# Hybrid decoder step: four prompt units inside each sample attention unit, with the sample keys turned half a unit earlier

## Time and profile before

| | us |
|---|---|
| median of 3 runs | 1231.96 (1231.15 to 1234.93) |
| the profiled execution, its own time | 1237.05 |
| span of the profiled execution | 1235.3 |

### The profile page before, as it was taken

How to read it: one execution, slowest core, us unless ns; L and a number is a source line. 1 busy time by engine, 2 the same in 40 slices (tenths; PEclk the granted TensorE clock), 3 DMA queues, 4 the chain that set the end, 5 groups by cost and what they waited for, 6 DMA issues and landing times.

```text
span 1235.3 us, 23971 instructions
## 1 busy us (share of the span) xinstructions
PE 1068.6 (87%) x9389; PEld 856.7 (69%) x9389; DVE 830.4 (67%) x1497; ACT 264.2 (21%) x588; POOL 350.1 (28%) x378
## 2 busy tenths in 40 slices
PE   5699899999688777778765996999999999999994
PEld 3377577666566555566544875999999999777772
DVE  1647346625778688777639577467676676998958
ACT  0300000012223323232233103332233232100002
POOL 0433123310000000000007005356664665434323
PEclk9799999985899889988886997999999999999997
DMA  8938989863599999998780216375567731413102
GB/s 293 408 135 328 359 329 349 301 238 108 197 366 352 340 344 373 370 327 295 279 305 1 64 38 210 136 266 211 205 232 278 270 105 69 148 57 104 69 19 77
DMA packets 112549, 276.54 MB, mean 224 GB/s; under 512 B 9608, under 2 KB 33174, under 8 KB 108837
## 3 DMA queue, kind: packets, MB, share of 16 engines
q1 hardware_dynamic: 100949, 254.52, 58.2%
q10 hardware_dynamic: 11488, 20.49, 5.0%
HBM read 264.60 MB, written 76.69 MB: 276 GB/s over the span
## 4 chain that ended last, share of the span: by engine, by line
PE 60%; DVE 15%; DMA 11%; ACTq 4%; issue 4%; SPq 2%; ACT 2%; POOL 1%; DVEq 0%; POOLq 0%; PEldq 0%
PE wide L1632 15%; PE wide L1634 15%; PE wide L1633 15%; DMA room<-in_cache_v 3%; PE wide L1768 3%; ACTq L481 3%; PE wide L1712 3%; PE wide L1701 2%; DMA x_sb<-in_cache_v 2%; DMA room<-in_w_ada 2%; DMA ring<-in_w_ada 2%; PE wide L1580 1%; DMA ring<-in_w_down 1%; DVE ring L1202 1%; PE wide L1706 1%
## 5 line engine op out<-in xcount | busy, mean ns | idle before, releaser
L782 POOL TENSOR_TENSOR ring_r<-ring,ring_r 128x1024 fp32r<-128x1024 f32 x70 | 184.6, 2645 | 286.5 <-DVE ring_r L1086 204.3
L1632 PE MATMUL wide<-x_sb_r,ring_r 128*128 128x288 f32 x704 | 211.3, 300 | 8.2 <-DVE ht_r L1108 5.2
L1633 PE MATMUL wide<-ht_r,ring_r 128*128 128x288 f32 x704 | 209.2, 297 | 0.0
L1634 PE MATMUL wide<-x_sb_r,ring_r 128*128 128x288 f32 x704 | 208.4, 296 | 0.0
L1634 PE MATMUL wide<-ring_r,ht_r 128*128 128x512 f32 (+1 forms) x400 | 158.9, 397 | 0.0
L1202 DVE STREAM_TRANSPOSE ring<-ring 128x512 f32<-128x512 f32 x208 | 129.9, 676 | 24.3 <-DMA ring<-in_cache_k 12.2
L1632 PEld LDWEIGHTS wide<-x_sb_r,ring_r 128*128 128x128 f32 x704 | 133.2, 189 | 11.7 <-issue 11.2
L1634 PEld LDWEIGHTS wide<-x_sb_r,ring_r 128*128 128x128 f32 x704 | 134.0, 190 | 0.0
L1633 PEld LDWEIGHTS wide<-ht_r,ring_r 128*128 128x128 f32 x704 | 133.6, 190 | 0.0
L1632 PE MATMUL wide<-ring_r,x_sb_r 128*128 128x512 f32 (+1 forms) x240 | 98.2, 409 | 10.1 <-DVE ht_r L1108 8.7
L770 POOL COPY x_sb<-ring 32x128 f32<-32x128 f32 x64 | 18.4, 287 | 286.4 <-PE wide L1768 284.3
(11 more groups left out here) (231 smaller groups left out, 1892.8 us busy)
## 6 DMA issues: line engine op xcount, KB each, us to landing
ring<-in_cache_k SPq DMA_DIRECT2D x128, 256.0 KB
out_wks<-in_cache_win_k SPq DMA_DIRECT2D x8, 4080.0 KB, 18.9
out_wvs<-in_cache_win_v SPq DMA_DIRECT2D x8, 4080.0 KB, 19.3
ring<-in_w_up SPq DMA_DIRECT2D x22, 1024.0 KB, 7.1
room<-in_w_ada SPq DMA_DIRECT2D x8, 2048.0 KB, 10.5
ring<-in_cache_win_k SPq DMA_DIRECT2D x16, 1024.0 KB
ring<-in_w_in SPq DMA_DIRECT2D x6, 2048.0 KB, 10.7
x_sb<-in_cache_win_v SPq DMA_DIRECT2D x40, 256.0 KB
```

The lines of the kernel that those rows point to most:

```text
L782: nc.gpsimd.tensor_tensor(rest, w, high.bitcast(F32), ALU.subtract).then_inc(wl_rest, 1)
L1632: nc.tensor.matmul(out, left[0], right[0], start=first, stop=False)
L1633: nc.tensor.matmul(out, left[0], right[1], start=False, stop=False)
L1634: return nc.tensor.matmul(out, left[1], right[0], start=False, stop=last)
```

## The change

It has five parts:

1. `NU` goes from 16 to 4 and `PER` from 3 to 4: twelve prompt units move from the front into the sample stage. Unit `w` of the first 15 sample units has four prompt units, the last one only the two closing steps.
2. The key turns move. In the front only the first group's four tiles are turned. In the loop, DVE turns groups 0, 1 and 2 of unit `w + 2` during unit `w` (`turn_new(w + 2)` among them), and group 3 of a page unit in the unit before its own.
3. On PE the transposes of the probabilities come first in a unit, ahead of the prompt step. The transposes of the new keys' probabilities come after both halves, with a semaphore of their own.
4. The new keys are scored after group 0 and masked by themselves (`mask_new`), ahead of the rest of the minimum (`least`). ACT makes the probabilities of unit `w + 1` during unit `w`, with prompt steps between.
5. SP loads the new values one iteration of its loop later, and in another place of it.

Cut to its core:

```diff
-        NU = 16
+        NU = 4
-        PER = len(pb) // (2 * DB)
+        PER = 4
@@ SP, loop over w @@
                 if w >= 2:
                     load_values(sp, w - 1, 0)
+                if w >= 3:
+                    sp.wait_ge(sa_pv, w - 2)
+                    load_new_values(sp, w - 2)
                 if here == 4:
                     load_keys(w, 3)
                 if w >= 2:
                     load_values(sp, w - 1, 1)
                     if sa[w - 1][0] == 0:
                         load_values(sp, w - 1, 2)
                 if here:
                     sp.wait_ge(kn_t, w)
                     load_new_keys(sp, w)
-                if w >= 2:
-                    sp.wait_ge(sa_pv, w - 1)
-                    load_new_values(sp, w - 1)
@@ ACT @@
+            def step_b(y):
+                if 1 <= y <= len(pb):
+                    copy_b(y - 1)
+                if y < len(pb):
+                    probs_b(y)
+            for w, (m, b) in enumerate(sa):
                 if w:
                     take_out(w - 1)
                 act.wait_ge(sa_t, 2 * w + 2)
                 if w >= 1:
                     act.wait_ge(sa_pv, w)
                 nc.scalar.activation(pt_s[:, 1, 0:full], bk(3)[:, 0:full], ACT.Copy).then_inc(sa_ph, 1)
+                step_b(PER * w)
                 if values_by_act(w, 3):
                     load_values(act, w, 3)
+                step_b(PER * w + 1)
+                if w + 1 < len(sa):
+                    probs_s(w + 1, 0)
+                    step_b(PER * w + 2)
+                    probs_s(w + 1, 1)
+                    if w + 2 < len(sa) and sa[w + 2][0] == 0:
+                        load_key_tail(act, w + 2)
+                    step_b(PER * w + 3)
+                    if values_by_act(w + 1, 2):
+                        load_values(act, w + 1, 2)
@@ DVE, front @@
-                if 1 <= s <= 8:
-                    turn_keys(0, (s - 1) // 4, ((s - 1) % 4,))
-                if s in (12, 14):
-                    turn_keys(0, 2, ((s - 12) // 2,))
+                if s >= 3:
+                    turn_keys(0, 0, (s - 3,))
@@ DVE, sample stage @@
+            def step_b(y):
+                if y < len(pb):
+                    mask_b(y)
+                if 2 <= y < len(pb) + 2:
+                    out_b(y - 2)
             dve.wait_ge(new_zero, 3)
             turn_new(0)
+            turn_keys(0, 1)
+            turn_keys(0, 2)
+            mask_new(0)
+            turn_keys(1, 0)
+            least(0)
+            turn_keys(1, 1)
+            turn_new(1)
+            turn_keys(1, 2)
+            for w, (m, b) in enumerate(sa):
...
                 nc.vector.tensor_copy(pt_s[:, 0, 0:full], bk(2)[:, 0:full]).then_inc(sa_pt, 1)
+                dve.wait_ge(sa_tn, w + 1)
                 nc.vector.tensor_copy(ptn[0:32, :, :], bk(4)[0:32, P:3 * P].rearrange("p (h c) -> p h c", h=2)).then_inc(sa_pt, 1)
+                step_b(PER * w)
+                if w + 1 < len(sa):
+                    mask_new(w + 1)
+                    if sa[w + 1][0] == 1:
+                        turn_keys(w + 1, 3)
+                    step_b(PER * w + 1)
+                    least(w + 1)
+                    step_b(PER * w + 2)
+                    if w + 2 < len(sa):
+                        turn_keys(w + 2, 0)
+                        turn_keys(w + 2, 1, (0, 1))
+                        turn_new(w + 2)
+                    step_b(PER * w + 3)
+                    if w + 2 < len(sa):
+                        turn_keys(w + 2, 1, (2, 3))
+                        turn_keys(w + 2, 2)
+                else:
+                    step_b(PER * w + 1)
@@ PE, after the transposes of unit w @@
+                last.then_inc(sa_tn, 1)
+                prompt_step(PER * w)
+                if w + 1 < len(sa):
+                    score_group(w + 1, 0)
+                    score_new(w + 1)
+                    score_group(w + 1, 1)
+                    pe.wait_ge(sa_nm, w + 2)
+                    prompt_step(PER * w + 1)
+                    for g in range(2, len(groups[sa[w + 1][0]])):
+                        score_group(w + 1, g)
+                    prompt_step(PER * w + 2)
                 else:
                     prompt_step(PER * w + 1)
                 pe.wait_ge(sa_pt, 2 * w + 2)
                 pe.wait_ge(sa_ph, w + 1)
                 for g in range(len(groups[m])):
                     weigh_group(w, g)
+                    if g == 1 and w + 1 < len(sa):
+                        prompt_step(PER * w + 3)
```

More of the change, by code:

```diff
@@ L767, in _ @@
                 if w >= 2:
-                    pool.wait_ge(sa_s, w - 1)
+                    pool.wait_ge(sa_g, NG[w - 1])
                 for i in range(4):
@@ L908, in take_out, with probs_s @@
                 nc.scalar.activation(o_s[:, w, :], bk(4)[:, 0:P], ACT.Copy).then_inc(sa_o, 1)
-            act.wait_ge(tail_zero, 1)
-            for w, (m, b) in enumerate(sa):
+            def step_b(y):
[3 more added lines that the diff above has]
+                    probs_b(y)
+            def probs_s(w, h):
+                m, b = sa[w]
                 n = 32 * sum(groups[m])
                 act.wait_ge(sa_min, w + 1)
[L914 to L930, removed]
@@ new lines, in probs_s @@
+                if w >= 1:
+                    act.wait_ge(sa_t, 2 * w)
+                    act.wait_ge(sa_tn, w)
+                src = sm_s[:, h, 0:n] if m == 0 else bk(h)[:, 0:n]
+                whole = P * (n // P)
+                tiled = p_s[:, h, 0:whole].rearrange("p (u m t) -> p u t m", m=32, t=4)
+                nc.scalar.activation(tiled, src[:, 0:whole].rearrange("p (u t m) -> p u t m", t=4, m=32), ACT.Exp,
+                                     bias=blk_o[:, h:h + 1], scale=-1.0, accum_out=rs_s[:, h, w:w + 1])
@@ new lines, in probs_s @@
+                if n > whole:
+                    rest = p_tail[:, h, :].rearrange("p (m t) -> p t m", t=4)[:, 0:2, :]
+                    nc.scalar.activation(rest, src[:, whole:n].rearrange("p (t m) -> p t m", m=32), ACT.Exp, bias=blk_o[:, h:h + 1], scale=-1.0,
+                                         accum_out=rs_x[:, h, w:w + 1])
+                nc.scalar.activation(p_s[:, h, n:n + 32], sm_n[:, h, :], ACT.Exp, bias=blk_o[:, h:h + 1], scale=-1.0,
+                                     accum_out=rs_n[:, h, w:w + 1]).then_inc(sa_exp, 1)
@@ L1282, in turn_new, with mask_new, least @@
                 if w >= 1:
-                    dve.wait_ge(sa_s, w)
+                    dve.wait_ge(sa_ns, w)
                 nc.vector.transpose(ktn[0:32, :, :], kn[0:32, :].rearrange("p (g d) -> p g d", d=32))\
                     .then_inc(kn_t, 1)
[L1287 to L1292, removed]
+            def mask_new(w):
+                m, b = sa[w]
+                dve.wait_ge(sa_ns, w + 1)
                 if w >= 1:
                     dve.wait_ge(sa_exp, 2 * w)
+                here = smask[:, 320 + 32 * m:352 + 32 * m]
+                then(nc.vector.tensor_tensor(sm_n, bk(7)[:, 384:448].rearrange("p (h n) -> p h n", h=2),
+                                             here[:, None, :].to_broadcast([P, 2, 32]), ALU.add))
+                nc.vector.tensor_reduce(blk[:, 2:4], sm_n, AX_X, ALU.min).then_inc(sa_nm, 1)
+            def least(w):
+                m, b = sa[w]
+                n = 32 * sum(groups[m])
+                dve.wait_ge(sa_g, NG[w + 1])
                 for h in range(2):
@@ L1301, in _ @@
                         then(nc.vector.tensor_reduce(blk[:, h:h + 1], bk(h)[:, 0:n], AX_X, ALU.min))
[L1302 to L1305, removed]
+                dve.wait_ge(sa_nm, w + 1)
                 then(nc.vector.tensor_tensor(blk[:, 0:2], blk[:, 0:2], blk[:, 2:4], ALU.min))
@@ L1802, in weigh_group @@
                 last.then_inc(sa_vg, 1)
-            for g in range(len(groups[0])):
-                score_group(0, g)
+            score_group(0, 0)
             score_new(0)
+            score_group(0, 1)
+            score_group(0, 2)
             for w, (m, b) in enumerate(sa):
                 n = 32 * sum(groups[m])
-                prompt_step(PER * w)
                 for h in range(2):
```

76 lines of the change are left out of this document (18 added, 58 removed).

## The result

| | before | after |
|---|---|---|
| median, us | 1233.45 (1231.15 to 1238.64, 4 runs) | 1340.19 (1336.10 to 1341.57, 4 runs) |
| the profiled execution, us | 1237.05 | 1336.1 |
| its span, us | 1235.3 | 1334.2 |

The ratio is 1.0854, 95% interval 1.0810 to 1.0897: slower by over 100 us, outside the predicted 1202 to 1284. Between the two profiled executions the loss is 99.05 us. A kernel now and then runs in a slower state, with a lower granted clock: medians and ranges here are over all of its runs, while ratios and their intervals leave such runs out.

What follows compares the result with a forecast made beforehand. It took DMA bytes to bound a unit pair (39.7 us), with the front on top. Front -22.5, seven pairs +53.9, last units -7.9, gap -4.7 gave +18.8 on 1237.05: 1255.9, as a median 1251; range 1202 to 1284.

Steps and rivals of the forecast that it cites:

- Part 4: DVE's `turn_new(w + 2)` waits for new keys behind SP's value loads: 7.3 us per page unit, 0.9 per window unit.
- P = 47.4: Sample stage: forecast time in us from start to start of a window and page unit pair, against 39.7 before.
- the walk: Step-by-step timing of a page and a window unit from their starts: next start at 27.0 and 20.4 us.
- Issue of the chain, 9.8: SP's queue in a page unit: issuing values, new values, page keys, more values and new keys, from 9.75 to 19.55.
- Landing, 1.8: New keys' DMA, end of issue to landed: taken as 1.8 us, between 0 and 3.6, as queues would be emptier.
- Part 1: The front before the sample stage shrinks: first start at 300.7, 22.5 us earlier than 323.2.
- Part 2: Twelve prompt units inside the sample stage: free by busy time, up to 22 us if the DMA cover goes.
- Part 3: Turning keys ahead on DVE: PE's 24.7 us of waits for turned keys go; a pair stays at 39.3.
- Part 5: SP's later new values in page units: cost nothing behind the late mask, up to 1.8 us a pair without it.
- The gap: Between the last sample product and the first operation behind the stage: 6.9 us falls to 2.2, a gain of 4.7.
- Rival C: Whole kernel slower by more, as PE's clock adds: pair near 49.5, 1265 us; chance 0.68 together with the forecast.
- Rival A: Sample stage: bytes still bound, a pair stays at 39.3, total change -37.9 to 1194 us; chance 0.22.

Runs made afterwards that it cites:

- experiment 1: Changed kernel, with SP loading the new keys ahead of the first value load: 1226.98 us, ratio 0.9978.
- experiment 4: Changed kernel, with DVE turning the new keys last in the unit, SP's order kept: 1285.89 us, ratio 1.0466.
- experiment 6: Changed kernel, with SP loading the new keys behind the first value group and new values, ahead of page key group 3: 1255.13 us.
- Experiment 2: Changed kernel, with ACT doing `take_out` ahead of its value loads: 1316.37 us, ratio 1.0724.
- experiment 3: Changed kernel, with SP's new keys ahead of the values and ACT's `take_out` ahead of its value loads: 1220.90 us, ratio 0.9915.
- experiment 5: Kernel of experiment 3, with 16 prompt units in the front again (`NU` back to 16, `PER` kept): 1242.94 us.
- Experiment 7: Kernel of experiment 3, with the new values also loaded ahead of value group 0: 1225.49 us.
- the fillers: Changed kernel plus unread PE products filling waits: 72 per window unit, ratio 1.1102; then 34 per window and 20 per page unit, ratio 1.0900.
- second filler kernel: Changed kernel plus unread PE products, 34 at the start of a window unit and 20 of a page unit: 1348.57 us, ratio 1.0900.
- experiment 11: Changed kernel, with SP and ACT reading page numbers into registers ahead of the buffer waits: 1328.35 us, ratio 1.0792.

## Why the prediction was wrong

**The sign and the mechanism were right, the size was not.** The step that fails is Part 4, "P = 47.4", and 70.5 of the 80.2 us that were missed lie in it (124.4 against 53.9). Even the dearest case that the prediction allowed, P = 52.4, lies below the measured 57.5: three terms of the walk were too small. The mechanism is the one that it named: DVE waits in every unit for the new keys of `w + 2` behind SP's value loads (experiments 1, 4 and 6), and the wait was to be "over 45 us in all"; it was 112.8.

Its own steps, for the page unit shown above:

- *Issue of the chain, 9.8.* It took 12.65. The register loads that read the page numbers stand between the new values' end and the first page key, 508.77 to 510.81: 2.0 that the walk left out. The earlier trace rows has such a gap, 393.74 to 395.34, but only the issues were added up; the choice between 1.9 and 3.3 for the page keys covered neither case, since gap and keys took 4.3 together. The rest is 0.3 each on the first value group and the page keys, and small gaps.
- *Landing, 1.8.* It took 3.2 here, and 2.5 to 3.8 in the fourteen units of the seven pairs (3.2 in the mean). My reason for halving the measured 3.6 of the earlier trace rows, that emptier queues land faster, was wrong in size: at a DMA share of 0.72 the landing is close to what it was at 0.99. The upper end of its bounds was the better value.
- *First value group at start + 9.75.* Its values were issued at + 12.9. DVE's second copy (L1351, 2.06 of waiting) is late, because PE's transposes at L1849 are, because ACT has issued four value DMAs in front of `take_out`. Experiment 2 puts 3.2 a pair on that. With them out of the way the values were issued at + 10.0, close to the walk. The walk had no ACT in it at all, since ACT is only 20% busy.
- *5.65 from landing to start.* It took 5.7.

Together 34.5 for the 27.0 that was forecast: 3.15 too little up to the first value issue, 2.85 in the chain, 1.4 in the landing. The window unit shown after it (start 526.60, next start 551.00) took 24.4 for 20.4: 11.3 to the first value group instead of 10.35, 8.3 to the landing instead of 5.6 (1.8 of it a gap of register loads ahead of the page values), 4.8 behind it.

**Part 1** held within 1 us, in part by luck: the front was over 5 us sooner than forecast (first group's last tile at 276.1, not 281.7), and DVE then waited 3.15 for the page keys and 3.87 for the new keys of unit 1 (timeline of DVE, kernel after):

```profile
276.09 0.70 DVE L1213 STREAM_TRANSPOSE ring<-ring 128x512 f32<-128x512 f32 x1
...
286.03 2.49 DVE L1213 STREAM_TRANSPOSE ring<-ring 128x512 f32<-128x512 f32 x4 [3.15 <-DMA ring<-in_cache_k]
...
296.83 0.70 DVE L1293 STREAM_TRANSPOSE ht<-ht 32x512 f32<-32x512 f32 x1 [3.87 <-DMA ht<-ring]
```

**Part 2**, the twelve units free inside the stage, is nearly borne out where the new keys are in time: experiments 3 and 5 put 3.4 us on them. What they cost while the wait lasts was not measured. **Part 3**: PE's waits for turned keys fell to 4.4 us. P without the wait was forecast as 39.3; it came out at 42.05 with the new keys early alone, and at 40.9 and 40.2 with ACT's order changed too. **Part 5** priced the new values at nothing behind the late mask. In the unit shown that was so: PE waited for them at 511.21 and then for `take_out` until 522.77. Experiment 7 shows nothing won by having them earlier.

**The last two units** were to take 31 and took 38.3. Unit 14 took 16.4 of the 17 forecast; unit 15 took 21.9 instead of 14. Its last page values come from ACT's queue, behind ACT's other work (issued from 726.92 to 730.38), and PE waited 7.69 us for them, until 7.8 after their issue (timeline of ACT's queue and PE, kernel after):

```profile
726.92 3.46 ACTq L481 DMA_DIRECT2D room<-in_cache_v  x4
...
738.16 1.91 PE L1825 MATMUL wide<-room,ht 128*16 128x128 f32 x32 [7.69 <-DMA room<-in_cache_v]
```

**The sentence of the Trainium skill on issuing** was misread. The prediction set all the issues of the earlier trace rows (fifteen there, it says sixteen) against one landing. Taken DMA by DMA the rows agree with it (0.71 against 3.6), and it says nothing that would make a pair 39.3.

**The gap** kept 5.3 of 6.9 instead of 2.2. **Rival C** had the direction: its 49.5 added a tenth on PE's terms for the clock, and the fillers show no such price behind the landing; ahead of the first value group it is open. **Rival A** would need the new keys in time: with that alone (experiment 1) the time is that of the kernel before (ratio 0.9978, the interval includes 1), and experiment 3, with ACT's order changed as well, lies 13.7 below it, not 37.9.

## What to carry to other kernels

When a wait moves from the end of one unit into another, follow the awaited transfer back through its issuing queue: a small urgent load behind gated bulk loads inherits their gates, and here three moved lines were worth some 110 us. Walk every in-order queue in such a chain, idle ones too (ACT, 20% busy, cost 3.2 a pair), with register loads and DMA issues as steps of their own. And a measured landing time is not scaled down on a guess about the load around it: here it stayed near 3 at a lower DMA share, and went to 4.8 in the window units of one experiment that had only moved the register loads.

## What the runs showed of the hardware

From the end of its issue to the start of its user, the small DMA of the new keys took 2.5 to 3.8 us in the changed kernel, at a DMA share of 0.72, and 3.6 in the one case of the earlier trace rows, at 0.99. In experiment 11, again at 0.72, it took 3.3 to 5.5.

PE's clock was low behind long waits; the table of stretches around the wait of the page unit, kernel after:

```profile
512.00:523.00 11.00, 0.65 (x6) 0.35 (x5) 1.97 (x9) 1.05 (x4) 0.00 (x0) 0.59 0.67 238
...
523.00:530.00 7.00, 6.57 (x95) 4.64 (x97) 6.01 (x15) 1.18 (x4) 0.00 (x0) 0.50 0.68 253
```

After 10 us of waiting PE ran the next 7 us at 0.50, its lower level (1.2 GHz); with the filler in the wait (second filler kernel) the clock stayed up:

```profile
520.00:530.00 10.00, 7.55 (x84) 6.41 (x83) 4.60 (x13) 1.53 (x5) 0.00 (x0) 1.00 0.50 168
```

Had I priced that clock as time behind the landing, it would have been a wrong term: the next start did not move.
